# GpSimd takes two of the eight tiles of each residual, and the samples' columns at the entry of a sublayer, in a two-layer decoder step

## The chip, the cores and the metric

One core of a Trainium2 chip runs the whole program. The metric is the device time of one execution in microseconds (us), lower is better. Engines are named as the profile names them: PE (TensorE, PEld its weight loads), DVE (VectorE), ACT (ScalarE), POOL (GpSimd), SP (SyncE, which issues the weight loads from HBM). A name with q is an engine's queue that issues DMAs.

## What is computed

Two layers of a decoder, on 256 prompt tokens and 8 sample tokens (one token each of 8 sequences) with the same weights, model width 1024, all in float32. Each layer has three sublayers, each between a norm at the entry and one at the exit:

```
def sub_in(t, i):
    return rmsnorm(t, norm_pre[i]) * (1.0 + m_scale[:, i, None]) + m_shift[:, i, None]

def sub_out(t, y, i, res):
    return t + res * m_gate[:, i, None] * rmsnorm(y, norm_post[i])

x = sub_out(x, swiglu(sub_in(x, 0), ffn_up[0], ffn_down[0]), 0, FFN_RES)
h = sub_in(x, 1)
...
x = sub_out(x, merged, 1, 1.0)
x = sub_out(x, swiglu(sub_in(x, 2), ffn_up[1], ffn_down[1]), 2, FFN_RES)
```

The middle sublayer projects h, runs two recurrent branches (RWKV-7 and gated DeltaNet) and merges them through w_out. The factors m_scale, m_shift and m_gate come from a conditioning vector: one for the whole prompt, one for each sample.

## The kernel before, in words

**Layout.** The state x is kept transposed in SBUF: xT has 128 partitions and 8 tiles (NT) of 264 columns (T), of which columns 0 to 255 (0:NPR) are the prompt's tokens and the last 8 (NPR:T) the samples'. A row of columns is a token, a partition of a tile one of the 1024 features. y (the output of a sublayer) and h (scratch for squares and scaled tiles) have the same shape. Weights arrive by DMA in a ring of five slots; ACT casts each to w_hi (`high`, line 714), DVE subtracts to get the low part (`low`, line 722), and each product is made of three matmuls (high x high, high x low, low x high), all on line 898.

**Order of work.** Every engine has its own program, written out by hand in the order in which it runs, and semaphores join them: nothing reorders at run time. Per layer: FFN 0, mixing, output projection, FFN 1. Names with "ada" are the matmuls that make the conditioning factors, spread in pieces over the program.

**The exit of a sublayer** (`sub_out(s)` on DVE; s is the sublayer). ACT evicts each output tile from PSUM to y, with the prompt's gate as the scale (`leave`), and squares it; PE sums the squares over the features (`mean_square`), ACT turns the sum into rs = (mean)^-1/2 by Ln and Exp (`normalise`, lines 1491 and 1493). DVE multiplies the samples' columns of y by their gates mod_g, waits for rs (`rs_ready`), and then does two operations for each of the eight tiles, interleaved by one: y = y\*rs, and xT = xT + y, which posts `x_ready`.

**The entry of the next sublayer** (`sub_in(s, hi)` on DVE). ACT squares each tile of xT as it is posted (`square_input`, line 1499), PE sums, ACT makes the new rs. At FFN 1 ACT also casts two weights between the squares and the new rs, and DVE splits them (`ahead`). DVE then makes for each tile scaled_x(j) = xT \* mod_a \* rs into h (256 prompt columns), ACT adds the shift and rounds to the high part hi ("cut", line 1514), and DVE makes the low part h_lo and posts `h_ready`; PE starts on tile k of the sublayer's first two products when h_ready for it is there (`enter`). The samples' eight columns of all tiles go through five operations of their own on DVE, in the buffer y[:, :, NPR:T] (`rows`): times mod_a, times rs, plus the shift, copy to hi, subtract to h_lo. The last four follow rs, and the first h_lo tile stands behind them:

```
tt(rows, rows, bm(rs[:, NPR:T], NT))
...
tt(rows, rows, bias[:, :, 1:NROW], ALU.add)
...
dve.tensor_copy(hi[:, :, NPR:T], rows)
...
tt(h_lo[:, :, NPR:T], rows, hi[:, :, NPR:T].bitcast(F32), ALU.subtract)
```

There are six residuals (three sublayers, two layers) and five entries that follow one; the very first entry has no residual ahead of it. Behind the last residual PE transposes xT back tile by tile (line 2581, and 2582 for the samples), and ACT and its queue write the outputs. `x_ready` counts all tiles, and X_DONE is its last count.

**POOL before.** At the start it sets constants (memsets, selects). Then, in each layer, it only issues DMAs for the mixing: `gather`, `fetch`, `store`, `scatter`, and loads of a recurrent state.

Of the kernel before, what the change touches and what calls it, by code (L numbers as in the profile page):

```python
# [55 lines left out]
X_DONE = 1 + 3 * DEPTH * NT  # L56
# [6 lines left out]
Y_BANKS = (4, 1)  # L63
B16 = 16
CLEAR0, INV0 = (29, 35, 67), (32, 38, 72)
SOLVE = ({21: (1, 4), 23: (4, 7), 24: (7, 10), 26: (10, 12), 27: (12, 15)}, {32: (1, 7), 33: (7, 15)}, {68: (1, 7), 69: (7, 15)})

# [126 lines left out]
def build(nc, I, O):  # L194
    ctx = ExitStack()
    with ctx:
# [532 lines left out]
        with nc.Block() as block:  # L729
# [139 lines left out]
            for l in range(DEPTH):  # L869

                @block.gpsimd
                def _(pool):
# [5 lines left out]

                    for run in range(3):
# [11 lines left out]
                    for g in range(2):  # L891
                        rows = I["state_rwkv_wkv"][l].rearrange("b (j g) v k -> g (b j) (v k)", g=2)[g]
                        pool.dma_start(samp_seen[64 * g:64 * g + 64, :, :].rearrange("p v k -> p (v k)"), rows[:, 2048:4096]).then_inc(samp_in[0].sem, samp_in[0].one())

                @block.tensor
                def _(pe):
# [23 lines left out]
                    def enter(outs, keys, x_hi):  # L920

                        both = [weights((l, *key)) for key in keys]
# [47 lines left out]
                    def mean_square(buf=h):  # L970

                        for k in range(NT):
                            pe.wait_ge(sq_ready.sem, sq_ready.next(pe))
                            i = mm(banks[0][:, 0:T], mean_all[:, :], buf[:, k, :], k == 0, k == NT - 1)
# [4 lines left out]
                    def ffn(i_ffn):  # L979
                        for t in range(FT):  # L980
                            if t == 0:
                                enter([banks[2 * g][:, 0:T] for g in range(2)], [(f"up{i_ffn}", g) for g in range(2)], hi_ffn)
# [45 lines left out]
                    else:  # L1028
                        mean_square()
                    ffn(0)  # L1030
                    mean_square()

                    def dense(t):
                        k = t
                        if k < 2:
                            if k == 0:
                                pe.wait_ge(out_taken.sem, out_taken.at(NT))
                                enter([banks[g][:, 0:T] for g in range(2)], TILES[0:2], hi_in)
# [392 lines left out]
                    mean_square()  # L1431
# [4 lines left out]
                def _(act):  # L1436
# [58 lines left out]
                    def square_input(start=False, m=None, late=False):  # L1495
                        for j in range(NT):
                            if j == 0 or not start:
                                act.wait_ge(x_ready.sem, x_ready.next(act))
                            act.activation(h[:, j, :], xT[:, j, :], ACT.Square).then_inc(sq_ready.sem, sq_ready.one())
                            if m and j == 6:  # L1500
# [479 lines left out]
                def _(dve):  # L1980
# [38 lines left out]
                    def sub_in(s, hi, shift_late=False):  # L2019
# [8 lines left out]
                        tt(rows, xT[:, :, NPR:T], mod_a[:, NT * s:NT * (s + 1), 1:NROW]).then_inc(dve_chain.sem, dve_chain.one())  # L2028
                        dve.wait_ge(dve_chain.sem, dve_chain.all())
# [4 lines left out]
                        tt(rows, rows, bm(rs[:, NPR:T], NT)).then_inc(dve_chain.sem, dve_chain.one())  # L2034
                        for j in range(1, NT if shift_late else 2):
                            scaled_x(j)
                        dve.wait_ge(dve_chain.sem, dve_chain.all())
                        if shift_late:
# [594 lines left out]
```

## Time and profile before

| | |
|---|---|
| time, median of 3 runs | 1984.1 us (1982.7 to 1984.65) |
| the profiled execution | 1987.61 us, its span 1985.9 us |
| mean granted TensorE clock | 0.965 |
| PE busy | 1857.3 us, 94% of the span |
| DVE busy | 1254.2 us, 63% |
| ACT busy | 927.1 us, 47% |
| POOL busy | 76.6 us, 4%, 155 instructions |
| DMA | 353.34 MB, mean 178 GB/s |

A share of busy time is a mean over stages of the program. Line numbers are those of the kernel before; most DVE work goes through two helpers (line 1982 for operations with two tensors, 1985 for those with a scalar per partition too), so groups are told apart by their tiles. A number in brackets at the end of a row is the time that the engine sat idle before it, and what ended that.

### The profile page before, as it was taken

What the parts mean: (1) busy time and instruction counts of PE and PEld (TensorE: products, weight loads), DVE (VectorE), ACT (ScalarE), POOL (GpSimd) and SP (SyncE); (2) the same over time, 40 slices, a digit from 0 to 9 for tenths busy, and PEclk for the clock granted to TensorE, in tenths of its full rate; (3) what the DMA queues carried; (4) which work ended last, traced back from release to release, by engine and by line L of the source; (5) the groups of instructions that cost most, each with busy time, mean ns of one, the idle gap of its engine ahead of it and who ended that gap; (6) DMA issues with size and microseconds to landing.
All of it is one profiled execution on the core that took longest, in us unless ns stands there. A gap on an engine that the chain in (4) does not pass through costs nothing.

```text
span 1985.9 us, 44909 instructions
## 1 busy us (share of the span) xinstructions
PE 1857.3 (94%) x19156; PEld 1685.2 (85%) x19156; DVE 1254.2 (63%) x2187; ACT 927.1 (47%) x1804; POOL 76.6 (4%) x155
## 2 busy tenths in 40 slices
PE   5999989999999888899999999899899998789998
PEld 3899978878888777788989999788799878679997
DVE  3455355776456776688656654577754586769953
ACT  3333455454456544433444444654544764353343
POOL 0000000121000200000000000001200011000000
PEclk7999999999999998999999999999999998899999
DMA  7777765655565664698765666554553555259873
GB/s 261 222 224 225 212 178 168 179 164 151 140 183 155 162 190 122 196 290 271 196 191 150 181 176 184 162 151 142 151 152 101 149 134 141 87 147 275 245 198 110
DMA packets 538085, 353.34 MB, mean 178 GB/s; under 512 B 19620, under 2 KB 515270, under 8 KB 536590
## 3 DMA queue, kind: packets, MB, share of 16 engines
q1 hardware_dynamic: 472202, 302.74, 53.2%
q10 hardware_dynamic: 60756, 38.81, 6.9%
q0 software_dynamic: 4928, 8.92, 1.7%
q8 instruction: 151, 2.47, 0.5%
q14 instruction: 48, 0.39, 0.1%
HBM read 332.27 MB, written 18.50 MB: 177 GB/s over the span
## 4 chain that ended last, share of the span: by engine, by line
PE 76%; DVE 10%; DMA 6%; ACT 4%; issue 3%; POOL 1%; SPq 0%; ACTq 0%; DVEq 0%; POOLq 0%
PE bank L898 73%; DMA ring<-in_w_ada 3%; DMA ring<-in_ffn_up 2%; PE bank L649 2%; DVE ring_r L722 2%; DVE far L1982 1%; ACT w_hi_r L714 1%; DVE y L1982 1%; DVE big L606 1%; DVE big L1982 1%; DVE big L605 1%; POOL far L625 1%; DVE h L1985 1%; DVE big L1985 1%; ACT far L614 0%
## 5 line engine op out<-in xcount | busy, mean ns | idle before, releaser
L898 PE MATMUL bank<-big_r,w_hi_r 128*128 128x264 f32 x4160 | 1074.2, 293 | 43.9 <-DVE h_r L1985 20.9
L898 PE MATMUL bank<-big_r,ring_r 128*128 128x264 f32 (+1 forms) x3456 | 992.1, 287 | 0.0
L898 PEld LDWEIGHTS bank<-big_r,w_hi_r 128*128 128x128 f32 x4160 | 744.8, 190 | 106.9 <-issue 86.0
L898 PE MATMUL bank<-h_r,w_hi_r 128*128 128x264 f32 x2752 | 792.1, 288 | 0.0
L722 DVE TENSOR_TENSOR ring_r<-ring,w_hi_r 128x1024 fp32r<-128x1024 f32 (+2 forms) x440 | 523.8, 1196 | 373.2 <-ACT w_hi_r L714 369.0
L714 ACT CAST w_hi_r<-ring 128x1024 fp32r<-128x1024 f32 (+2 forms) x440 | 452.6, 1029 | 458.7 <-PE bank L898 231.0
L898 PEld LDWEIGHTS bank<-big_r,ring_r 128*128 128x128 f32 (+1 forms) x3456 | 657.9, 190 | 1.1
L898 PEld LDWEIGHTS bank<-h_r,w_hi_r 128*128 128x128 f32 x2752 | 527.9, 192 | 1.6 <-issue 0.5
L898 PE MATMUL bank<-ring,c 128*32 128x256 f32 x1152 | 94.4, 407 | 24.4 <-DMA ring<-in_w_ada 23.9
L898 PE MATMUL bank<-big,far 64*64 64x64 f32 (+2 forms) x1440 | 103.7, 255 | 0.0
L898 PEld LDWEIGHTS bank<-big,far 64*64 64x64 f32 (+1 forms) x1440 | 86.9, 139 | 11.9 <-issue 11.3
L1982 DVE TENSOR_TENSOR big<-big,bank 128x264 f32<-128x264 f32 (+2 forms) x138 | 62.7, 458 | 36.5 <-PE bank L898 24.6
L898 PEld LDWEIGHTS bank<-ring,c 128*32 128x32 f32 x1152 | 24.1, 110 | 55.2 <-DMA ring<-in_w_ada 33.8
L898 PE MATMUL bank<-big 128*64 128x64 f32 (+4 forms) x736 | 52.4, 273 | 18.6 <-DVE big L1982 18.6
L570 POOL DMA_DIRECT2D lt_blocks<-far x48 | 26.9, 568 | 1017.4 <-issue 642.1
L898 PEld LDWEIGHTS bank<-big 128*64 128x64 f32 (+2 forms) x736 | 39.1, 166 | 30.9 <-DVE big L1982 22.1
L649 PE MATMUL bank<-far 64*64 64x48 f32 (+2 forms) x1536 | 54.0, 226 | 9.7 <-DMA far<-t_blocks 8.2
L649 PEld LDWEIGHTS bank<-far 64*64 64x64 f32 x1536 | 51.1, 145 | 13.5 <-DMA far<-t_blocks 8.9
L1985 DVE SCALAR_TENSOR_TENSOR rs<-big,pcol,rs 128x256 f32<-128x256 f32 x78 | 37.8, 485 | 37.3 <-ACT rs L1656 35.1
L898 PE MATMUL bank<-far 64*64 64x64 f32 (+1 forms) x864 | 54.6, 233 | 0.7 <-DVE far L664 0.7
L1599 ACT COPY big<-bank 128x264 f32<-128x264 f32 x48 | 18.2, 380 | 78.1 <-PE bank L898 77.8
L898 PEld LDWEIGHTS bank<-far 64*64 64x64 f32 (+1 forms) x864 | 51.0, 146 | 3.7 <-DVE far L664 0.9
(300 smaller groups left out, 1827.7 us busy)
## 6 DMA issues: line engine op xcount, KB each, us to landing
ring<-in_ffn_up SPq DMA_DIRECT2D x176, 512.0 KB, 4.6
ring<-in_w_in SPq DMA_DIRECT2D x148, 512.0 KB, 3.9
ring<-in_w_ada SPq DMA_DIRECT2D x144, 512.0 KB, 4.3
ring<-in_ffn_down SPq DMA_DIRECT2D x64, 512.0 KB, 3.8
far<-in_state_gdn_ssm ACTq DMA_DIRECT2D x28, 512.0 KB, 5.5
ring<-in_ffn_down SPq DMA_DIRECT2D x32, 384.0 KB, 3.2
ring<-in_w_out SPq DMA_DIRECT2D x16, 512.0 KB, 4.3
out_sample_gdn_ssm<-far ACTq DMA_DIRECT2D x16, 512.0 KB, 4.7
```

What stands on the lines that cost most here:

```text
L570: pool.dma_start(lt_blocks[part_of, :, :].rearrange("u s t -> s u t"), lt[rows, :, cols]).then_inc(block_in.sem, block_in.one())
L605: after(dve.tensor_tensor(p, t_s.to_broadcast([P, rest, s]), t_m[:, s:s + 1, 0:s].to_broadcast([P, rest, s]), ALU.mult))
L606: after(dve.tensor_tensor(below, below, p, ALU.add))
L625: pool.dma_start(into[rows, :, 2 * cols.start:2 * cols.stop], t_blocks[part_of].rearrange("u s t w -> s u (t w)")).then_inc(block_out.sem, ...
L649: i = pe.matmul(out, x_b[hf, u, :] if s else lt[hf, u, :], moving, start=True, stop=True)
L714: act.copy(w_hi[:, m % HI, 0:size], ring[:, slot[n], 0:size]).then_inc(hi_ready.sem, hi_ready.one())
L722: dve.tensor_tensor(ring_r[:, slot[n], 0:size], w, w_hi[:, m % HI, 0:size].bitcast(F32), ALU.subtract).then_inc(lo_ready.sem, lo_ready.one())
L898: return pe.matmul(out, lhsT, rhs, start=start, stop=stop)
L1599: act.copy(qk[:, i - A_TILES, 3:T + 3], src)
L1982: return dve.tensor_tensor(out, a, b, op)
L1985: return dve.scalar_tensor_tensor(out, a, s, b, op0, op1)
```

## The change

In each residual DVE does tiles 0 to 5 (LATE = 6) and POOL tiles 6 and 7, with its own semaphores. At the five entries behind a residual POOL does the five operations on the samples' columns; the first entry keeps them on DVE. ACT and PE take the squares in the order 0, 1, 2, 6, 3, 4, 5, 7. PE's `enter` first waits for POOL's last operation. `pooled(l, what, n)` counts what POOL has posted. The core of the diff:

```
+LATE = NT - 2
+SQUARED = (0, 1, 2, 6, 3, 4, 5, 7)
-X_DONE = 1 + 3 * DEPTH * NT
+X_DONE = 1 + 3 * DEPTH * LATE
...
+                    def residual(s):
+
+                        pool.wait_ge(out_taken.sem, out_taken.at((NT, NT + PROJ + NT, NT + PROJ + 2 * NT)[s]))
+                        ys = y[:, LATE:NT, NPR:T]
+                        pool.tensor_tensor(ys, ys, mod_g[:, NT * s + LATE:NT * (s + 1), 1:NROW], ALU.mult).then_inc(pool_chain.sem, pool_chain.one())
+                        pool.wait_ge(pool_chain.sem, pool_chain.all())
+                        pool.wait_ge(rs_ready.sem, rs_ready.at(2 * s + 2))
+                        for j in range(LATE, NT):
+                            pool.tensor_tensor(y[:, j, :], y[:, j, :], rs[:, :], ALU.mult).then_inc(pool_chain.sem, pool_chain.one())
+                            pool.wait_ge(pool_chain.sem, pool_chain.all())
+                            pool.tensor_tensor(xT[:, j, :], xT[:, j, :], y[:, j, :], ALU.add).then_inc(pool_done.sem, pool_done.one())
+
+                    def rows_in(s, hi):
+
+                        sub = s % 3
+                        rows, bias = y[:, :, NPR:T], modv[:, 3 * NT * sub:3 * NT * sub + NT, 1:NROW]
+
+                        def then(i):
+                            i.then_inc(pool_chain.sem, pool_chain.one())
+                            pool.wait_ge(pool_chain.sem, pool_chain.all())
+
+                        pool.wait_ge(x_ready.sem, x_ready.nth(1 + LATE * (3 * l + s)))
+                        pool.wait_ge(pool_done.sem, pool_done.all())
+                        then(pool.tensor_tensor(rows, xT[:, :, NPR:T], mod_a[:, NT * sub:NT * (sub + 1), 1:NROW], ALU.mult))
+                        pool.wait_ge(rs_ready.sem, rs_ready.at(2 * s + 1))
+                        then(pool.tensor_tensor(rows, rows, bm(rs[:, NPR:T], NT), ALU.mult))
+                        then(pool.tensor_tensor(rows, rows, bias, ALU.add))
+                        then(pool.tensor_copy(hi[:, :, NPR:T], rows))
+                        pool.tensor_tensor(h_lo[:, :, NPR:T], rows, hi[:, :, NPR:T].bitcast(F32), ALU.subtract).then_inc(pool_done.sem, pool_done.one())
+
+                    residual(0)
+                    rows_in(1, hi_in)
                     for run in range(3):
...
+                    residual(1)
+                    rows_in(2, hi_ffn)
+                    residual(2)
+                    if l + 1 < DEPTH:
+                        rows_in(3, hi_ffn)
...
+                    def enter(outs, keys, x_hi, rows=None):
+
+                        if rows:
+                            pe.wait_ge(pool_done.sem, pool_done.nth(rows))
...
-                        for j in range(NT):
-                            if j == 0 or not start:
+                        for n, j in enumerate(range(NT) if start else SQUARED):
+                            if j >= LATE and not start:
+                                act.wait_ge(pool_done.sem, pool_done.nth(pooled(m[0], ("out", m[1]), j - LATE)))
+                            elif n == 0 or not start:
                                 act.wait_ge(x_ready.sem, x_ready.next(act))
...
                         dve.wait_ge(x_ready.sem, x_ready.all())
-                        tt(rows, xT[:, :, NPR:T], mod_a[:, NT * s:NT * (s + 1), 1:NROW]).then_inc(dve_chain.sem, dve_chain.one())
-                        dve.wait_ge(dve_chain.sem, dve_chain.all())
+                        if not shift_late:
+                            dve.wait_ge(pool_done.sem, pool_done.nth(pooled(l if s else l - 1, ("out", (s - 1) % 3), 1)))
...
-                        ys = y[:, :, NPR:T]
-                        tt(ys, ys, mod_g[:, NT * s:NT * (s + 1), 1:NROW]).then_inc(dve_chain.sem, dve_chain.one())
+                        ys = y[:, 0:LATE, NPR:T]
+                        tt(ys, ys, mod_g[:, NT * s:NT * s + LATE, 1:NROW]).then_inc(dve_chain.sem, dve_chain.one())
...
-                        for j in range(NT + 1):
-                            if j < NT:
+                        for j in range(LATE + 1):
+                            if j < LATE:
```

How it moves instructions. DVE before, at the end of layer 0's first residual and the entry to the mixing:

```order
L1982 TENSOR_TENSOR y<-y,rs 128x264
L1982 TENSOR_TENSOR xT<-xT,y 128x264 [waits dve_chain] x2
L1982 TENSOR_TENSOR y<-xT,mod_a 128x8x8 [waits x_ready]
L1985 SCALAR_TENSOR_TENSOR h<-xT,mod_a,rs 128x256 [waits rs_ready,dve_chain]
L1982 TENSOR_TENSOR y<-y,rs 128x8x8
L1985 SCALAR_TENSOR_TENSOR h<-xT,mod_a,rs 128x256
L1982 TENSOR_TENSOR y<-y,modv 128x8x8 [waits dve_chain]
L2044 CAST big_r<-y 128x8x8 [waits dve_chain]
L1982 TENSOR_TENSOR h_r<-y,big_r 128x8x8 [waits dve_chain]
L1985 SCALAR_TENSOR_TENSOR h_r<-h,modv,big_r 128x256 [waits cut_ready]
```

Here big_r holds hi, h_r is h_lo, and modv the shift. The same place on DVE in the changed kernel (its line numbers differ):

```order
L2035 TENSOR_TENSOR y<-y,rs 128x264
L2035 TENSOR_TENSOR xT<-xT,y 128x264 [waits dve_chain] x2
L2038 SCALAR_TENSOR_TENSOR h<-xT,mod_a,rs 128x256 [waits rs_ready,pool_done,x_ready]
L2038 SCALAR_TENSOR_TENSOR h<-xT,mod_a,rs 128x256
L2038 SCALAR_TENSOR_TENSOR h_r<-h,modv,big_r 128x256 [waits cut_ready]
```

The five operations of 128x8x8 have left, and four of the 128x264 ahead of them. They stand on POOL, ahead of the layer's first gather, where before there was no instruction:

```order
L894 TENSOR_TENSOR y<-y,mod_g 128x2x8 [waits out_taken]
L898 TENSOR_TENSOR y<-y,rs 128x264 [waits rs_ready,pool_chain]
L900 TENSOR_TENSOR xT<-xT,y 128x264 [waits pool_chain]
L898 TENSOR_TENSOR y<-y,rs 128x264
L900 TENSOR_TENSOR xT<-xT,y 128x264 [waits pool_chain]
L913 TENSOR_TENSOR y<-xT,mod_a 128x8x8 [waits pool_done,x_ready]
L915 TENSOR_TENSOR y<-y,rs 128x8x8 [waits rs_ready,pool_chain]
L916 TENSOR_TENSOR y<-y,modv 128x8x8 [waits pool_chain]
L917 CAST big_r<-y 128x8x8 [waits pool_chain]
L918 TENSOR_TENSOR h_r<-y,big_r 128x8x8 [waits pool_chain]
L581 DMA lt_blocks<-far 16x16x16 [waits prod_dve]
```

All but one wait for the one in front; only the second y\*rs starts without a wait.

## Rows read from the trace of the kernel before

**Rows 1.** The page: the chain by engine, and the costliest group of instructions

```profile
PE 76%; DVE 10%; DMA 6%; ACT 4%; issue 3%; POOL 1%; SPq 0%; ACTq 0%; DVEq 0%; POOLq 0%
...
L898 PE MATMUL bank<-big_r,w_hi_r 128*128 128x264 f32 x4160 | 1074.2, 293 | 43.9 <-DVE h_r L1985 20.9
```

**Rows 2.** Windows over three of the five edges: length, then busy time per engine

```profile
263.00:278.05 15.05, 10.28 (x59) 6.07 (x58) 9.07 (x29) 6.90 (x17) 0.00 (x0) 1.00 0.69 200
...
1034.50:1047.22 12.72, 8.26 (x48) 3.90 (x46) 9.51 (x31) 6.08 (x14) 0.00 (x0) 0.96 0.54 156
...
1753.00:1767.37 14.37, 6.99 (x24) 3.63 (x24) 10.20 (x27) 7.87 (x16) 0.00 (x0) 0.97 0.28 74
```

**Rows 3.** Timeline, first residual: start us, duration us, engine, line, operation, tiles

```profile
267.34 0.42 ACT L1493 ACTIVATE rs<-rs 128x264 f32<-128x264 f32 x1
...
267.87 0.78 DVE L1982 TENSOR_TENSOR y<-y,rs 128x264 f32<-128x264 f32 x2 [3.46 <-ACT rs L1493]
268.56 0.42 DVE L1982 TENSOR_TENSOR xT<-xT,y 128x264 f32<-128x264 f32 x1
...
269.08 0.42 ACT L1499 ACTIVATE h<-xT 128x264 f32<-128x264 f32 x1 [1.32 <-DVE xT L1982]
...
272.69 0.77 DVE L1982 TENSOR_TENSOR xT<-xT,y 128x264 f32<-128x264 f32 x2
...
273.15 0.77 ACT L1499 ACTIVATE h<-xT 128x264 f32<-128x264 f32 x2 [0.26 <-DVE xT L1982]
```

**Rows 4.** Timeline, the entry behind it, up to the first matmul

```profile
275.33 0.42 ACT L1493 ACTIVATE rs<-rs 128x264 f32<-128x264 f32 x1
275.86 0.49 DVE L1985 SCALAR_TENSOR_TENSOR h<-xT,mod_a,rs 128x256 f32<-128x256 f32 x1 [2.14 <-ACT rs L1493]
...
276.40 0.48 DVE L1985 SCALAR_TENSOR_TENSOR h<-xT,mod_a,rs 128x256 f32<-128x256 f32 x1
276.44 0.98 ACT L1514 ACTIVATE big_r<-h,modv 128x256 fp32r<-128x256 f32 x2 [0.69 <-DVE h L1985]
...
277.28 0.22 DVE L1982 TENSOR_TENSOR h_r<-y,big_r 128x64 fp32r<-128x64 f32 x1
277.42 0.48 DVE L1985 SCALAR_TENSOR_TENSOR h_r<-h,modv,big_r 128x256 fp32r<-128x256 f32 x1
...
278.05 0.44 PE L898 MATMUL bank<-big_r,w_hi_r 128*128 128x264 f32 x1 [3.27 <-DVE h_r L1985]
```

**Rows 5.** Timeline of POOL at the program's start

```profile
3.68 0.32 POOL L757 MEMSET carry<- 128x264 f32 x1
4.06 0.10 POOL L759 MEMSET carry<- 128x4 f32 x1
...
5.19 0.53 POOL L740 TENSOR_SCALAR_AFFINE_SELECT masks<-masks 64x64 f32<-64x64 f32 x2
5.79 0.23 POOL L740 TENSOR_SCALAR_AFFINE_SELECT below<-below 64x48 f32<-64x48 f32 x1
```

**Rows 6.** Timeline, last residual: DVE's adds and PE's transposes of tiles 5 to 7

```profile
1978.52 0.43 DVE L1982 TENSOR_TENSOR xT<-xT,y 128x264 f32<-128x264 f32 x1
...
1979.01 0.68 PE L2581 MATMUL bank<-ident,xT 128*128 128x128 f32 x2
...
1979.70 0.68 PE L2581 MATMUL bank<-ident,xT 128*128 128x128 f32 x2
...
1980.39 0.63 PE L2581 MATMUL bank<-ident,xT 128*128 128x128 f32 x2
```

**Rows 7.** Timeline, entry to layer 0's second FFN: weight splits ahead of the first scaled_x

```profile
806.22 2.36 DVE L722 TENSOR_TENSOR ring_r<-ring,w_hi_r 128x1024 fp32r<-128x1024 f32 x2 [1.24 <-ACT w_hi_r L714]
...
807.48 0.42 ACT L1493 ACTIVATE rs<-rs 128x264 f32<-128x264 f32 x1
808.50 0.48 DVE L1985 SCALAR_TENSOR_TENSOR h<-xT,mod_a,rs 128x256 f32<-128x256 f32 x1
```

**Rows 8.** Windows, behind the first matmul: length, busy per engine, PE clock, DMA share, GB/s

```profile
278.05:281.36 3.31, 3.31 (x15) 3.31 (x16) 3.31 (x9) 2.04 (x4) 0.00 (x0) 0.52 0.00 0
```

More of the change, by code:

```diff
@@ L66, with pooled @@
 SOLVE = ({21: (1, 4), 23: (4, 7), 24: (7, 10), 26: (10, 12), 27: (12, 15)}, {32: (1, 7), 33: (7, 15)}, {68: (1, 7), 69: (7, 15)})
+def pooled(l, what, n=0):
+    steps = [("out", 0), ("out", 0)] + [("in", 1)] * 1 + [("values", 0)] * 0
+    steps += [("out", 1), ("out", 1)] + [("in", 2)] * 1 + [("out", 2), ("out", 2)] + [("in", 3)] * 1
+    kind = ("values", 0) if what == "values" else what
+    return POOL_SETUP + l * len(steps) + steps.index(kind) + (n if what == "values" else steps.count(kind) - 1 if n is None else n) + 1
 class Signal:
@@ L1037, in dense @@
                                 pe.wait_ge(out_taken.sem, out_taken.at(NT))
-                                enter([banks[g][:, 0:T] for g in range(2)], TILES[0:2], hi_in)
+                                enter([banks[g][:, 0:T] for g in range(2)], TILES[0:2], hi_in, pooled(l, ("in", 1)))
                             return
@@ L1430, in _ @@
                     edge_begins(1)
-                    mean_square()
+                    mean_square(order=SQUARED)
                     ffn(1)
@@ L2033, in sub_in @@
                         scaled_x(0)
[L2034 removed]
+                        if shift_late:
+                            tt(rows, rows, bm(rs[:, NPR:T], NT)).then_inc(dve_chain.sem, dve_chain.one())
                         for j in range(1, NT if shift_late else 2):
                             scaled_x(j)
[L2037 removed]
                         if shift_late:
+                            dve.wait_ge(dve_chain.sem, dve_chain.all())
                             for m in range(2):
@@ L2041, in sub_in @@
                             conditioning(0, 1, sel_shift_ready)
-                        tt(rows, rows, bias[:, :, 1:NROW], ALU.add).then_inc(dve_chain.sem, dve_chain.one())
-                        dve.wait_ge(dve_chain.sem, dve_chain.all())
-                        dve.tensor_copy(hi[:, :, NPR:T], rows).then_inc(dve_chain.sem, dve_chain.one())
-                        dve.wait_ge(dve_chain.sem, dve_chain.all())
-                        tt(h_lo[:, :, NPR:T], rows, hi[:, :, NPR:T].bitcast(F32), ALU.subtract)
+                            tt(rows, rows, bias[:, :, 1:NROW], ALU.add).then_inc(dve_chain.sem, dve_chain.one())
+                            dve.wait_ge(dve_chain.sem, dve_chain.all())
+                            dve.tensor_copy(hi[:, :, NPR:T], rows).then_inc(dve_chain.sem, dve_chain.one())
+                            dve.wait_ge(dve_chain.sem, dve_chain.all())
+                            tt(h_lo[:, :, NPR:T], rows, hi[:, :, NPR:T].bitcast(F32), ALU.subtract)
                         for j in range(NT):
```

25 lines of the change are left out of this document (16 added, 9 removed).

## The prediction

> **What bounds the kernel now.** I read the page first, its chain and its groups: TensorE (PE) carries 76% of the chain that ended last, VectorE (DVE) 10%, and the largest group of matmuls sat idle 43.9 us, of which it waited 20.9 us for the tile h_r that DVE writes [rows 1]. So most of the span is PE work that this change doesn't touch, and DVE is on the path only in places. The places are the six residuals and the five entries behind them. The windows view, laid over the stretch from the last matmul of one sublayer to the first of the next, gives 12.7 to 15.1 us for each of the five, with PE busy in only half to two thirds of it [rows 2]. The timeline of the first one shows why: it is a chain with nothing beside it.
>
> Residual: the factor rs is ready at 267.34 + 0.42 = 267.76. DVE starts at 267.87 and issues 16 operations of 128x264, eight y\*rs and eight xT+y, at a pace of (5.59 - 0.43)/15 = 0.344 us (an operation lasts 0.43, the next starts before it ends), and ends at 272.69 + 0.77 = 273.46. ScalarE (ACT) squares each tile 0.04 us behind its add; the first adds leave gaps, the last two squares run together and the last one starts at about 273.50 [rows 3]. Entry: PE sums the squares, ACT makes the new rs (ready 275.75), DVE starts the first scaled_x at 275.86, and the first matmul of the sublayer comes at 278.05, 2.30 us behind rs [rows 4]. In these 2.3 us the five small operations on the samples' columns stand between the scaled tiles and the first h_lo, of which four come behind rs. Behind the first matmul PE is the slower side: it runs for 3.31 us at a granted clock of 0.52 (the 1.2 GHz level, after a stretch in which it only summed squares), busy all the time [rows 8]. So what matters is when it starts.
>
> **The change, part by part.** GpSimd (POOL) does nothing at these places now, so only the new work counts there. Its DMAs are issued in the same order, and those of the mixing wait for things that come microseconds behind an entry; I cost that at nothing. The small gate operations on the samples (y\*mod_g) run before rs is ready, on DVE and on POOL: nothing.
>
> *(a) Four of sixteen operations leave DVE, in each of six residuals.* DVE's last add ends at 267.87 + 11 x 0.344 + 0.43 = 272.08. The square of tile 5 follows at 272.12, that of tile 7, now last, 0.35 later: 272.47 for 273.50, **-1.03 us**, if POOL is done by then and DVE keeps its pace. In the last residual the adds feed transposes, and those take 0.69 us a tile even where the tile is long there (1979.70, 1980.39) [rows 6]. PE is as slow as DVE there, so I take -0.1 without a slower DVE, and -0.35 (one slot, for tile 5) as the start from which delays count.
>
> *(b) The same four operations on POOL, in a chain.* No row has POOL with two inputs. Bounds for one of 128x264: 0.32 us, its memset of that size, which only writes; and 0.75 us, three accesses (two reads, one write) at the memset's slope of (0.32 - 0.10)/260 = 0.82 ns a column, 3 x 264 x 0.82 = 0.65, and its fixed 0.10 [rows 5]. I take 0.6, nearer the upper, since operations that read are slower in the same rows than memsets. With a gap of 0.07 four take 2.7 us and end near 270.6, before DVE. POOL's own length thus costs nothing; tile 7 is in time up to (272.43 - 267.91)/4 = 1.13 us each.
>
> *(c) Both engines read SBUF at the same moment.* This is the term that decides and that no row shows. All 12 operations left on DVE and all 4 on POOL read two operands from SBUF. Call d the delay that one POOL operation puts on DVE's row of operations. At least 0: they run side by side. At most 0.75 + 0.08 = 0.83: DVE waits for the whole operation and loses its own overlap of 0.43 - 0.344. A residual costs -1.03 + 4d, the last one -0.35 + 4d, so the whole change is zero near d = 0.2, one quarter of the interval. I take **d = 0.5**: the two take turns, and DVE waits for the part of POOL's 0.6 in which it moves data (less the fixed 0.10). Five residuals: 5 x (-1.03 + 2.0) = +4.85; the last: +1.65.
>
> The Trainium skill ("SBUF — State Buffer", section "Who interferes with whom") says of this that a VectorE instruction with two SBUF inputs contends with a GpSimd instruction that reads SBUF, and that the one which starts second "fully blocks"; no run here shows it. By that rule alone d would be at its upper part; without it the sum would be that of the first rival.
>
> *(d) The samples' operations at five entries.* Four leave the 2.30 us. On DVE the path is then scaled_x (start +0.11, 0.49), ACT's cut (start 276.44, 0.69 behind rs, 0.51 long by half of the pair's 0.98 and its overlap), h_lo (0.48), and PE 0.15 behind it: 0.69 + 0.51 + 0.48 + 0.15 = 1.83, or **-0.47**. PE now waits for POOL's last one as well. POOL's four, at the pace of its select of 64x64 (0.30 [rows 5]), take 1.2: side by side they are hidden. In turns, each may wait for a DVE operation of 0.48: at worst 0.11 + 1.2 + 1.92 + 0.15 = 3.38, +1.1. I take half of the waits: 0.26 + 1.2 + 0.96 = 2.42, and DVE's path, delayed by two of POOL's, is 1.83 + 0.60 = 2.43: **+0.15**, five times +0.75.
>
> *(e) The waits.* At the second FFN's entry DVE now waits for POOL's tile 7 ahead of its two weight splits; these wait for ACT's casts, which come behind all squares anyway [rows 7]. They move with (a): DVE is the last there (808.50, rs was ready at 807.90), and the chain is as long as before. ACT and PE take tile 6 fourth; at 0.35 us a square it fits a gap.
>
> The sum: 4.85 + 1.65 + 0.75 = **+7.25 us**. The profiled execution took 1987.61 us (1.7 of it outside the span of 1985.9); it would become 1994.9. It stood 3.5 above the median of the runs, 1984.1, and against that the prediction is 1991.4. Ends: side by side 5 x (-1.03 - 0.47) - 0.1 = -7.6; whole blocking 5 x (2.29 + 1.08) + 2.97 = +19.8.
>
> **The rivals.** A measurement of this kernel tells from no change about 0.2%, 4 us.
>
> *Side by side.* d = 0, all of (a) and (d) is gained: 1976.5. For it: POOL is idle, each engine keeps to other columns, and nothing in the profile shows one disturbing the other. Against it: nothing shows them reading together either. It decides at d under 0.2, and is the rival that ends on the other side.
>
> *POOL is the bound.* They run side by side, but an operation takes POOL over 1.13 us, and tile 7 and the samples' columns come last: at 1.39 each ((273.46 - 267.91)/4) a residual gains nothing, and an entry nothing at 0.51 for a small one. At 1.3 and 0.5 the time is 5 x -0.36 - 0.1 = -1.9, 1982.2. Against it: it needs more than the 0.75 of my upper bound; for it: a first two-input operation on POOL after hundreds of microseconds of DMA issuing is a case that no row shows.
>
> *Given back.* The 1 to 1.5 us of an edge are regained or lost elsewhere, since the weights come no earlier. Against it: the loads of the next tiles are in before the entry starts, and PE is busy without a break behind it [rows 8]. I count it into the second rival's middle.
>
> **How the numbers follow.** Taking turns 0.50, side by side 0.32, POOL the bound or given back 0.18. Of the first, slower by over 4 us (d above 0.36 or so) 0.42, within it 0.07, faster 0.01; of the second, faster 0.28, within 0.04; of the third, within 0.11, slower 0.06, faster 0.01. So faster 0.30, same 0.22, slower 0.48. The range goes from just under the side-by-side value, 1976, to 2001 (+17; most of the way to whole blocking), which leaves out some 0.08 at each end. The likeliest case alone would be 1985 to 2001.
>
> **What would show it.** In the changed profile: the pace of DVE's operations in a residual while POOL works (0.344 now; about 0.34 + 0.5 per POOL operation if they take turns); POOL's lengths (0.6, or stretched to over 1); the start of the last square behind rs (5.74 now; 6.7 by the forecast, 4.71 side by side); the first matmul behind the second rs (2.30 now; 2.45, or 1.83); its releaser, POOL or DVE; and the last add of DVE against POOL's. The prediction is wrong if DVE's pace stays 0.344 with POOL beside it.

## The result, and the profile of the changed kernel

The changed kernel takes 1995.4 us (median of 19 runs, 1987.6 to 2002.1) against 1984.1 (19 runs, 1975.3 to 1992.7): the ratio is **1.0065 [1.0051, 1.008]**, slower by 10 to 16 us. The profiled execution took 1991.18 us, its span was 1989.5. The page, as [rows 1]:

```profile
PE 72%; DVE 12%; DMA 6%; ACT 5%; issue 3%; POOL 1%; ACTq 1%; SPq 0%; DVEq 0%; POOLq 0%
...
L946 PE MATMUL bank<-big_r,w_hi_r 128*128 128x264 f32 x4160 | 1071.5, 292 | 43.5 <-DVE ring_r L733 13.1
...
L946 PE MATMUL bank<-h,mean_all 128*128 128x264 f32 x160 | 53.6, 498 | 11.5 <-ACT h L1552 11.5
```

DVE has a larger share of the chain, 12% for 10%. PE's idle time in the large group is the same, 43.5 for 43.9 us, but h_r no longer ends most of it. So the loss isn't in that group. It shows in the timeline of the first residual, as [rows 3], its columns the same:

```profile
266.63 0.42 ACT L1544 ACTIVATE rs<-rs 128x264 f32<-128x264 f32 x1
...
267.16 1.32 DVE L2035 TENSOR_TENSOR y<-y,rs 128x264 f32<-128x264 f32 x2 [3.42 <-ACT rs L1544]
267.21 0.99 POOL L898 TENSOR_TENSOR y<-y,rs 128x264 f32<-128x264 f32 x1 [3.53 <-ACT rs L1544]
268.27 0.82 POOL L900 TENSOR_TENSOR xT<-xT,y 128x264 f32<-128x264 f32 x1
268.41 0.97 DVE L2035 TENSOR_TENSOR xT<-xT,y 128x264 f32<-128x264 f32 x1
...
270.06 0.81 POOL L900 TENSOR_TENSOR xT<-xT,y 128x264 f32<-128x264 f32 x1
270.19 0.97 DVE L2035 TENSOR_TENSOR xT<-xT,y 128x264 f32<-128x264 f32 x1
271.08 0.42 DVE L2035 TENSOR_TENSOR y<-y,rs 128x264 f32<-128x264 f32 x1
...
271.67 6.35 PE L946 MATMUL bank<-h,mean_all 128*128 128x264 f32 x14 [1.01 <-ACT h L1552]
...
272.80 0.77 DVE L2035 TENSOR_TENSOR xT<-xT,y 128x264 f32<-128x264 f32 x2
273.25 1.08 ACT L1552 ACTIVATE h<-xT 128x264 f32<-128x264 f32 x3 [0.26 <-DVE xT L2035]
...
278.06 0.48 ACT L1542 ACTIVATE rs<-bank,epsc 128x264 f32<-128x264 f32 x1 [3.72 <-PE bank L946]
```

While POOL works, DVE's operations last 0.97 us instead of 0.42 and follow each other by 0.89 instead of 0.344. The sixth starts at 271.08, 3.92 us behind the first, where it would start after 5 x 0.344 = 1.72: the four POOL operations delay DVE by 2.2 us, 0.55 each. From there on the pace is 0.344 again. The last add ends at 272.80 + 0.77 = 273.57, 6.51 behind rs (ready at 267.05) for 5.70 before, the squares at 274.33. Then comes what the prediction didn't hold: ACT's next operation waits 3.72 us for PE's sums (0.90 before), and starts 11.01 behind the first rs, where it started 7.06 behind it. The windows over the stages of this edge show what changed for PE (length, PE, its weight loads, DVE, ACT and POOL busy, granted clock, DMA share, GB/s):

```profile
267.16:271.67 4.51, 1.35 (x10) 0.46 (x11) 4.51 (x7) 0.85 (x2) 3.51 (x4) 0.91 0.95 264
271.67:278.05 6.38, 6.35 (x14) 4.49 (x14) 1.90 (x6) 2.20 (x6) 0.32 (x1) 0.53 0.25 87
278.05:281.11 3.06, 0.00 (x1) 0.03 (x1) 1.78 (x4) 1.82 (x4) 1.32 (x4) 1.00 0.00 0
281.11:284.40 3.29, 3.29 (x15) 3.29 (x16) 3.29 (x9) 2.05 (x4) 0.00 (x0) 0.50 0.00 0
```

PE worked 1.35 of the 4.51 us in which the slowed DVE released two tiles, and then summed at a granted clock of 0.53 (most of it at the 1.2 GHz level). In the same stretch of the other four edges the clock was 0.55, 0.58, 0.68 and 0.64. Before, it was 1.00 while PE summed (270.00 to 275.30).

The entry, as [rows 4], and the entry to the last FFN:

```profile
279.14 1.05 DVE L2038 SCALAR_TENSOR_TENSOR h<-xT,mod_a,rs 128x256 f32<-128x256 f32 x2 [5.57 <-ACT rs L1544]
279.14 0.32 POOL L915 TENSOR_TENSOR y<-y,rs 128x64 f32<-128x64 f32 x1 [5.18 <-ACT rs L1544]
...
280.37 0.32 POOL L918 TENSOR_TENSOR h_r<-y,big_r 128x64 fp32r<-128x64 f32 x1
280.38 0.59 DVE L2038 SCALAR_TENSOR_TENSOR h_r<-h,modv,big_r 128x256 fp32r<-128x256 f32 x1 [0.19 <-ACT big_r L1567]
...
281.11 0.54 PE L946 MATMUL bank<-big_r,w_hi_r 128*128 128x264 f32 x1 [3.09 <-DVE h_r L2038]
...
1767.22 0.39 PE L946 MATMUL bank<-big_r,w_hi_r 128*128 128x264 f32 x1 [3.24 <-POOL h_r L918]
```

Here rs is ready at 278.99 and the first matmul follows 2.12 us later (2.30 before). At both entries to the second FFN POOL ends last and the first matmul comes 2.26 us behind rs (2.78 before; there DVE shares the time with two weight splits). POOL's groups:

```profile
L898 POOL TENSOR_TENSOR y<-y,rs 128x264 f32<-128x264 f32 x12 | 11.5, 962 | 21.3 <-ACT rs L1544 21.3
...
L900 POOL TENSOR_TENSOR xT<-xT,y 128x264 f32<-128x264 f32 x12 | 9.7, 811 | 0.9
```

The five edges, from the first rs to the first matmul of the next sublayer, take 14.06, 14.00, 13.46, 12.63 and 13.08 us (10.29, 11.65, 10.29, 10.27 and 11.64 before): **+13.1 us**. Of these 5 x 1.12 = 5.6 lie ahead of the end of the squares, 9.0 between that and the start of ACT's Ln (the time of PE's sums; at a second FFN ACT's casts also lie in it), and 3 x -0.18 + 2 x -0.51 = -1.6 behind the second rs. In the last residual DVE ends only 0.82 us later, but from rs to the end of the span it is 13.4 for 11.6 us, and PE's transposes are slow from the first on:

```profile
1978.38 0.69 PE L2641 MATMUL bank<-ident,xT 128*128 128x128 f32 x2 [3.42 <-DVE xT L2035]
...
1980.16 0.69 PE L2641 MATMUL bank<-ident,xT 128*128 128x128 f32 x2 [0.88 <-DVE xT L2035]
```

Before, the first four pairs had lasted 0.44 and only the later ones 0.63 to 0.69. In all +14.9 us by the rows, for the measured 10 to 16. The two profiled spans differ by 3.6 only: between two edges there are hundreds of microseconds that this change doesn't touch, and they vary. The longest such stretch (first to second edge) took 521.0 us in the profile of before, 512.0 in that of after, and 513 to 523 in those of the experiments below. So each edge is read in the profile and the total in the repeated runs.

### The profile page after: what moved, and what is told of

The parts are those of the page before. It is cut to its first block, busy times and chain, and to the rows that moved or that the text cites. A ratio compares the mean times of both kernels' runs of the same rounds, so it can differ in the third digit from the quotient of the medians.

```text
span 1989.5 us, 44936 instructions
## 1 busy us (share of the span) xinstructions
PE 1845.7 (93%) x19156; PEld 1676.8 (84%) x19156; DVE 1255.0 (63%) x2138; ACT 926.9 (47%) x1804; POOL 108.6 (5%) x210
## 4 chain that ended last, share of the span: by engine, by line
PE 72%; DVE 12%; DMA 6%; ACT 5%; issue 3%; POOL 1%; ACTq 1%; SPq 0%; DVEq 0%; POOLq 0%
PE bank L946 70%; DMA ring<-in_ffn_up 3%; DMA ring<-in_w_ada 2%; DVE ring_r L733 2%; PE bank L660 2%; DVE y L2035 1%; ACT w_hi_r L725 1%; DVE big L2035 1%; DVE far L2035 1%; DVE big L617 1%; POOL far L636 1%; DVE big L616 1%; ACTq L1918 1%; DVE h L2038 1%; DVE big L2038 1%
## 5 line engine op out<-in xcount | busy, mean ns | idle before, releaser
L946 PE MATMUL bank<-big_r,w_hi_r 128*128 128x264 f32 x4160 | 1071.5, 292 | 43.5 <-DVE ring_r L733 13.1
L946 PE MATMUL bank<-h,mean_all 128*128 128x264 f32 x160 | 53.6, 498 | 11.5 <-ACT h L1552 11.5
L946 PEld LDWEIGHTS bank<-h,mean_all 128*128 128x128 f32 x160 | 38.4, 250 | 25.9 <-ACT h L1552 17.6
## 6 DMA issues: line engine op xcount, KB each, us to landing
ring<-in_ffn_up SPq DMA_DIRECT2D x176, 512.0 KB, 4.6
ring<-in_w_in SPq DMA_DIRECT2D x148, 512.0 KB, 3.9
ring<-in_w_ada SPq DMA_DIRECT2D x144, 512.0 KB, 4.3
ring<-in_ffn_down SPq DMA_DIRECT2D x64, 512.0 KB, 3.7
far<-in_state_gdn_ssm ACTq DMA_DIRECT2D x28, 512.0 KB, 6.1
ring<-in_w_out SPq DMA_DIRECT2D x16, 512.0 KB, 4.4
out_sample_gdn_ssm<-far ACTq DMA_DIRECT2D x16, 512.0 KB, 4.9
```

The costliest lines, as they stand in the source:

```text
L946: return pe.matmul(out, lhsT, rhs, start=start, stop=stop)
```

## The experiments

The theory after this result was: DVE and POOL hold each other up when both read SBUF; the slowed DVE leaves gaps in PE's work; PE's clock falls, and the sums are slow. The rivals: the entries or PE's added wait cost the time; the cost lies in POOL working at all, whatever it reads; the lower clock comes along with the loss and costs nothing itself. Where an edge is measured below, it runs from the first rs ready to the first matmul; the five together took 54.1 us before and 67.2 after the change.

### Each half of the change alone

Residuals alone: POOL keeps its two tiles, DVE takes the samples' operations back, and PE's wait goes.

```diff
                     residual(0)
-                    rows_in(1, hi_in)
...
                     residual(1)
-                    rows_in(2, hi_ffn)
                     residual(2)
-                    if l + 1 < DEPTH:
-                        rows_in(3, hi_ffn)
```

> The change with the residuals' part alone: POOL takes tiles 6 and 7 of each residual, the samples' columns at the entries are back on DVE. Theory (the loss lies in the residual: DVE and POOL take turns at reading, and the longer gaps let PE's clock fall while it sums the squares): DVE's first five operations of a residual still take 3.9 us instead of 1.7, the last square ends about 7.3 us behind rs, the sums end late (new factor started 9.6 to 11 us behind rs, 7.06 before), and the entry is as before, 2.30 us from the second rs to the first matmul (2.78 at the second FFN). Sum of the edges' excess 15 to 17 us, ratio 1.006 to 1.009. Rival (PE's wait for POOL at the entry makes the loss): edges as before and ratio within 0.2% of 1.

Measured: **1.0072 [1.0046, 1.0099]** (8 runs against 29). The edges sum to 66.0 us, DVE ends 6.50 and the squares 7.27 us behind rs, as with the whole change; behind the second rs it is 2.29 again at three entries. With the last residual (13.7 for 11.6) the excess is 14.0 us, just under the 15 to 17 expected. One of its edges, the second, tells the delay and the clock apart. There matmuls for the conditioning factors ran in the gap, PE's clock stayed at 1.00, and the sums of equally late squares were fast:

```profile
797.75:802.37 4.62, 2.39 (x27) 0.62 (x19) 4.51 (x7) 0.85 (x3) 3.51 (x4) 1.00 0.62 177
...
802.37 3.67 PE L941 MATMUL bank<-h,mean_all 128*128 128x264 f32 x14 [1.01 <-ACT h L1546]
...
806.82 0.47 ACT L1536 ACTIVATE rs<-bank,epsc 128x264 f32<-128x264 f32 x1
```

The fourteen matmuls take 3.67 us where they took 6.14 in the changed kernel's second edge, and Ln starts 1.79 us behind the end of the squares, as in the kernel before (there ACT's casts end last in both; in the changed kernel it is 3.50).

Entries alone: all eight tiles stay on DVE, POOL does the samples' operations.

```diff
-LATE = NT - 2
-SQUARED = (0, 1, 2, 6, 3, 4, 5, 7)
+LATE = NT
+SQUARED = (0, 1, 2, 3, 4, 5, 6, 7)
...
-                    residual(0)
                     rows_in(1, hi_in)
```

> The change with the entries' part alone: all eight tiles of a residual on DVE, the five small operations on the samples' columns on POOL. Theory (residual makes the whole loss): residual and sums as before (last square ends 6.16 us behind rs, PE at full clock while it sums), the first matmul follows the second rs by 2.12 us instead of 2.30, and by 2.26 instead of 2.78 at the second FFN: 1.5 us in all, ratio 0.999, not to be told from 1. Rival (POOL's small operations and PE's wait for them cost something): edges longer than before, ratio above 1.002.

Measured: **1.0002 [0.9984, 1.002]** (10 against 29). The edges sum to 53.1 us, 1.1 less than before; the first matmul comes 2.12 us behind rs (2.51 at the second FFN, where 2.26 was expected). So the whole loss comes with the residuals. The entries gain about 1 us, which a total can't show.

### POOL beside DVE on spare data

What does POOL's work cost DVE, if it is no part of the computation's chain? The kernel before, with four extra operations on POOL beside the first residual of each layer, from the constant tile carry into a spare buffer. The output is the same.

```diff
+                    pool.wait_ge(rs_ready.sem, rs_ready.at(2))
+                    for j in range(4):
+                        i = pool.tensor_tensor(svx[:, 0:T], carry[:, :], carry[:, :], ALU.mult)
...
+                                pe.wait_ge(pool_done.sem, pool_done.nth(4 + l))
                                 enter([banks[g][:, 0:T] for g in range(2)], TILES[0:2], hi_in)
```

> The kernel before, and beside each layer's first residual POOL does four operations of 128x264 with two inputs in SBUF (constants into a spare place, results unused), each waiting for the one in front; DVE keeps all 16 operations. Theory (turns at reading): DVE loses 0.5 to 0.6 us per POOL operation, so its last add ends 7.9 us behind rs instead of 5.70, and POOL's operations take 0.8 to 1.0 us. Rival (what slows DVE is that both work on the same tiles and semaphores of the residual): DVE ends at 5.70.

The second kernel has `pool.tensor_copy(svx[:, 0:T], carry[:, :])` in that place, which reads one operand:

> As beside_tt_b, with copies of 128x264 (one input in SBUF). If any read by POOL makes DVE's two-input operations wait, DVE ends 0.2 to 0.5 us later per copy, so between 6.5 and 7.7 us behind rs, less than beside two-input operations because a copy is shorter. Rival (only POOL's second input collides): 5.70.

The third has `pool.memset(svx[:, :], 1.0)`, 896 columns each, which only writes:

> As beside_tt_b, with memsets of 128x896 (no input, written data only, some 0.85 us each by the slope of the memsets at the program's start). Theory (the collision is in reading): DVE ends at 5.70 us behind rs, as if POOL were idle. Rival (any POOL operation that touches SBUF blocks DVE): 3 us later.

The timelines of the three, two inputs first:

```profile
266.31 2.95 POOL L881 TENSOR_TENSOR svx<-carry 128x264 f32<-128x264 f32 x4 [260.14 <-ACT rs L1501]
266.33 1.67 DVE L1990 TENSOR_TENSOR y<-y,rs 128x264 f32<-128x264 f32 x2 [3.46 <-ACT rs L1501]
267.92 0.85 DVE L1990 TENSOR_TENSOR xT<-xT,y 128x264 f32<-128x264 f32 x1
...
269.47 0.42 DVE L1990 TENSOR_TENSOR xT<-xT,y 128x264 f32<-128x264 f32 x1
```

One input:

```profile
266.12 2.05 POOL L881 COPY svx<-carry 128x264 f32<-128x264 f32 x4 [259.95 <-ACT rs L1501]
266.16 1.20 DVE L1990 TENSOR_TENSOR y<-y,rs 128x264 f32<-128x264 f32 x2 [3.46 <-ACT rs L1501]
267.28 0.62 DVE L1990 TENSOR_TENSOR xT<-xT,y 128x264 f32<-128x264 f32 x1
...
268.38 0.42 DVE L1990 TENSOR_TENSOR xT<-xT,y 128x264 f32<-128x264 f32 x1
```

None:

```profile
266.70 3.55 POOL L881 MEMSET svx<- 128x896 f32 x4 [260.61 <-ACT rs L1501]
266.75 0.78 DVE L1990 TENSOR_TENSOR y<-y,rs 128x264 f32<-128x264 f32 x2 [3.46 <-ACT rs L1501]
267.44 0.42 DVE L1990 TENSOR_TENSOR xT<-xT,y 128x264 f32<-128x264 f32 x1
```

DVE's last add ends 7.44, 6.53 and 5.69 us behind rs, against 5.70 without POOL, and the same to 0.01 us in the second layer. So an operation of two inputs delays DVE by 1.75/4 = 0.44 us, one of one input by 0.21, and a memset by nothing, though four of them keep POOL busy for 3.55 us. The first two delays are smaller than expected (0.5 to 0.6 for two inputs), and so are POOL's own operations: 0.63 to 0.70 us with two inputs, which are here one and the same tile, where 0.8 to 1.0 was expected, and 0.40 to 0.49 for a copy. There is one run of each, and their times of 1986.9, 1978.4 and 1978.5 us are inside the spread of single runs (before: 1977.5 to 1988.9) and settle nothing. The delay doesn't come from POOL working, and it doesn't need the residual's own tiles: it comes with POOL's reads.

### The clock: filler for PE in the gaps

The changed kernel, with seven matmuls on constants into an unused bank, four ahead of PE's wait for the first square and three ahead of the second.

```diff
                         for n, k in enumerate(order):
+                            for _ in range((4, 3)[n] if fill and n < 2 else 0):
+                                mm(banks[1][:, 0:T], mean_all[:, :], carry[:, :], True, True)
                             pe.wait_ge(sq_ready.sem, sq_ready.next(pe))
```

> The changed kernel with seven more matmuls on PE at each entry (constants, into a free bank, results unused): four ahead of the first square and three ahead of the second, so that PE has work in the gaps that slower squares leave. Theory (of the 15 us that the edges lose, about 9 come from PE's clock, which fell to 0.5 while it waited between squares): with the gaps filled the granted clock stays at 1.00 while PE sums, the new factor starts about 0.9 us behind the last square instead of 2.3 to 3.7, edges lose 5 to 7 us in all and the ratio is 1.002 to 1.004. Rival (the sums are slow for another reason, the extra matmuls only add work): the sums stay slow and the ratio is 1.006 or more.

Measured: **1.0074 [1.0052, 1.0096]** (10 against 29). Windows over the first edge and the 5 us behind it:

```profile
267.21:279.08 11.87, 7.54 (x42) 5.80 (x39) 8.19 (x16) 4.85 (x13) 5.15 (x9) 0.97 0.50 152
279.08:284.08 5.00, 5.00 (x23) 5.00 (x24) 4.82 (x13) 3.27 (x7) 0.00 (x0) 0.50 0.00 0
```

The clock in the five edges is 0.97, 1.00, 1.00, 0.99 and 0.87 (0.72 to 0.86 without the filler), the squares end as late as before (7.28), and Ln starts 8.3 to 9.8 us behind rs instead of 9.6 to 11.0. The edges sum to 61.3 us, 5.9 less than with the change alone. So the low clock did make the sums slow. That 5.9 and not all 9.0 us come back is at least in part the filler's own doing: in the second edge the second square is there at 805.00, but its sum starts at 806.96, behind the filler. Ln was expected 0.9 us behind the last square and starts 1.0 to 2.6 behind it.

But the time didn't follow. The ratio is what the rival forecast, and the lower end of its interval, 1.0052, is above what the edges would give, (14.9 - 5.9)/1984 = 0.45%. The gain isn't lost right behind the entries, although at two of them (the fourth and fifth) PE ran at 1.00 in the changed kernel and at 0.68 and 0.66 with the filler: from an edge's first Ln to ACT's first weight cast behind its entry the five edges together take 89.1 us before, 101.4 with the change and 95.5 with the filler. At that cast all of the 5.9 us are still there. Whether and where they are lost later, these runs don't settle.

### DVE reads one operand from PSUM

If the delay is in reads of SBUF, it should go when DVE reads only one of its two operands there. In five of the six residuals ACT writes the factor into PSUM too (banks[1]), DVE puts y\*rs into three free banks in turn, and adds from there. POOL keeps its tiles and reads SBUF. The last residual stays as it was.

```diff
+                            act.activation(banks[1][:, 0:T], rs[:, :], ACT.Exp, scale=-0.5).then_inc(rs_ready.sem, rs_ready.one())
+                            act.activation(rs[:, :], rs[:, :], ACT.Exp, scale=-0.5).then_inc(rs_ready.sem, rs_ready.one())
...
-                                tt(y[:, j, :], y[:, j, :], rs[:, :]).then_inc(dve_chain.sem, dve_chain.one())
+                                tt(product[j], y[:, j, :], factor).then_inc(dve_chain.sem, dve_chain.one())
...
-                                tt(xT[:, j - 1, :], xT[:, j - 1, :], y[:, j - 1, :], ALU.add).then_inc(x_ready.sem, x_ready.one())
+                                tt(xT[:, j - 1, :], xT[:, j - 1, :], product[j - 1], ALU.add).then_inc(x_ready.sem, x_ready.one())
```

> The changed kernel, but in five of the six residuals (all but the last) no DVE operation has two operands in SBUF: ACT writes the factor rs to a PSUM bank first and to SBUF behind it, DVE writes y*rs to PSUM banks and adds from there. POOL's part is unchanged. Theory (DVE and POOL wait for each other only because both read two operands from SBUF): DVE keeps a pace of 0.34 to 0.42 us per operation while POOL works, the last square ends 5.2 to 5.9 us behind rs (6.16 in the kernel before, 7.28 in the changed one), PE keeps its clock, and the ratio to the kernel before is 0.996 to 1.000. Rival (any operation of POOL beside DVE slows it, whatever DVE reads): the first five operations take 3.9 us as now, ratio 1.006 or more.

Measured: 0.9989 [0.9972, 1.0006] (10 against 29). The timeline of the first residual:

```profile
266.50 0.78 DVE L2042 TENSOR_TENSOR bank<-y,bank 128x264 f32<-128x264 f32 x2 [3.39 <-ACT bank L1576]
266.88 0.74 POOL L898 TENSOR_TENSOR y<-y,rs 128x264 f32<-128x264 f32 x1 [3.83 <-ACT rs L1577]
267.18 0.42 DVE L2042 TENSOR_TENSOR xT<-xT,bank 128x264 f32<-128x264 f32 x1
...
268.58 3.85 PE L946 MATMUL bank<-h,mean_all 128*128 128x264 f32 x16
...
269.90 0.76 DVE L2042 TENSOR_TENSOR xT<-xT,bank 128x264 f32<-128x264 f32 x2
...
272.47 0.48 ACT L1542 ACTIVATE rs<-bank,epsc 128x264 f32<-128x264 f32 x1 [1.04 <-PE bank L946]
```

DVE's pace beside POOL is 0.340 us, and POOL takes 0.74 and 0.75 an operation, reading the same tiles from SBUF. The last add ends 3.92 us behind the SBUF rs, the sums run at a clock of 1.00, and Ln starts 5.73 behind rs (7.06 before, 11.01 after the change). The edges sum to 46.2 us, counted from the SBUF rs. That one is ready 0.33 us behind the PSUM one, so this count leaves out 1.7 us over five edges. A second set of runs, since the interval included no change:

> The same kernel as psum_after_b, to see whether its gain over the kernel before is real: edges 6 us shorter, ratio 0.997 with an interval below 1 if the edges' gain reaches the end; within 0.1% of 1 if it is given back.

Measured: 0.9982 [0.9962, 1.0003] (10 against 21). One edge, 10.69 us, was longer: PE waited for the weights of an ada piece.

The control has the same operands in PSUM and no work on POOL: the kernel before with the two edits above, over all eight tiles.

> The kernel before with the PSUM operands of psum_after_b and without any work on POOL: a control. Theory (PSUM operands only make room for POOL, DVE's pace is the same): DVE's 16 operations at 0.344 us, last add 5.5 us behind the first operation, ratio 0.999 to 1.001. Rival (the gain of psum_after_b comes from the PSUM operands themselves): edges shorter by over 1 us each, as there.

Measured: 1.0003 [0.9986, 1.0021] (10 against 13), DVE's pace 0.340. The edges sum to 53.3 us by the same count (one of them, 11.14, had late weights too). So PSUM as an operand gains nothing by itself. It takes away what POOL costs, and then POOL's share of the work shortens the edges by 7.1 us against this control. In the time the two sets with POOL, 0.9989 and 0.9982, don't show that gain clear of no change, each by itself.

### The same at the entries: the fastest version

DVE's scaled_x also reads two operands from SBUF, while POOL does the samples' columns. Here the entry's factor goes to PSUM too.

```diff
-                            stt(h[:, j, 0:NPR], xT[:, j, 0:NPR], mod_a[:, NT * s + j, 0:1], rs[:, 0:NPR],
+                            stt(h[:, j, 0:NPR], xT[:, j, 0:NPR], mod_a[:, NT * s + j, 0:1], banks[3][:, 0:NPR],
```

> As psum_after_b, and the factor rs of the entries is in PSUM too, so that scaled_x no longer reads two operands from SBUF beside POOL's small operations. Theory: the first scaled_x takes 0.48 us again, h_lo follows earlier and the first matmul comes 1.9 us behind the SBUF copy of the second rs's Exp start-to-end as before, or 0.2 to 0.3 us earlier per edge than in psum_after_b, unless POOL's last small operation (1.7 us behind rs) is then the later one; edges 6 to 8 us shorter in all than in the kernel before, ratio 0.996 to 0.999. Rival (gain of the edges is given back in the stages behind them): edges shorter and ratio 1.000 or more.

Measured: **0.9972 [0.9955, 0.999]** (12 against 21; 1975.7 us for 1982.0). The first matmul comes 1.65 to 1.70 us behind the SBUF rs, 2.09 and 2.34 at the second FFNs. The edges sum to 45.9 us. This beats both the kernel before and the changed one: the whole of split residuals, samples' operations on POOL and factors in PSUM is worth having. There is no control with the entries' factor in PSUM and POOL idle, so the last step's own share isn't shown. The windows of its first entry, 5 us and the 15 behind them:

```profile
275.19:280.19 5.00, 5.00 (x29) 5.00 (x30) 4.82 (x13) 3.44 (x7) 0.00 (x0) 0.68 0.00 0
280.19:295.19 15.00, 14.40 (x121) 12.59 (x122) 8.12 (x12) 10.44 (x21) 0.00 (x0) 1.00 0.73 211
```

### Is the low clock behind an entry worth anything?

The fastest version, with six filler matmuls behind each edge's sums, while ACT and DVE prepare the entry.

```diff
                         mean_square(order=SQUARED)
+                        warm()
                     ffn(0)
```

> The kernel of psum_all with six more matmuls on PE behind the sums of each of the five later entries (constants, into a free bank, results unused; 0.47 us each at full clock), in the 3 us in which PE waits for the factor and the first tile. Theory (PE's clock falls behind an entry because PE stood still ahead of it, as it fell within the sums of the changed kernel): the granted clock of the first 5 us behind the first matmul is over 0.9 instead of 0.66, 1.5 us less per edge, ratio 0.993 to 0.996. Rival (the clock falls whatever PE does there, or the extra matmuls run at the low clock themselves and delay the first real one): the stretch behind stays at 0.66 or the first matmul comes up to 2.6 us later, ratio 0.998 to 1.004.

Measured: 1.0006 [0.9986, 1.0026] (12 against 17), against 0.9972 without the filler. The same windows:

```profile
276.52:281.52 5.00, 5.00 (x40) 4.99 (x41) 4.82 (x13) 3.45 (x7) 0.00 (x0) 1.00 0.00 0
281.52:296.52 15.00, 13.13 (x111) 11.36 (x111) 8.19 (x12) 10.44 (x22) 0.00 (x0) 1.00 0.75 211
```

The forecast of 0.993 to 0.996 failed. The clock is 1.00 behind all five entries and PE gets through 40 matmuls instead of 29 in the 5 us. But in the next 15 us it is busy for 13.1 instead of 14.4: it arrives earlier at weights that come no sooner. Their preparation starts with DVE's last h_lo tile, ACT's load of a function table and its first cast, and from an edge's first Ln to that cast it is 83.2 us over the five edges, 81.9 without the filler. The edges themselves are 1.6 us longer (47.5), none of it behind the filler: in the first one PE waited for the weights of an ada piece, and in the fifth it had stood still for 2.72 us and then summed at a clock of 0.71. The clock was made full and nothing was won. Why it rather came out slower than the fastest version (the intervals overlap, on another chip) stays open, as with the filler above.

## Why the prediction was right or wrong

The sign and the case were right: the engines hold each other up at SBUF, and the kernel is slower. It came out at 1995.4 for 1991.4 us, +11.3 in the medians (10 to 16 by the ratio) for +7.25. That it is so near is in part luck: the sum lacks a term larger than itself, and the time fell inside the range because the range reached up to nearly whole blocking, which is not what happened. By its steps:

- **(c), the deciding term, held.** The delay per POOL operation was put at 0.5 us within 0 to 0.83; it is 0.55 in this kernel and 0.44 on spare data. The start of the last square was forecast 6.7 us behind rs and is 6.9. Five residuals up to the squares' end: +4.85 forecast, +5.6 measured. The Trainium skill ("SBUF — State Buffer", section "Who interferes with whom") says that a VectorE instruction with two SBUF inputs contends with a GpSimd instruction that reads SBUF, not with one that only writes, and that with at most one SBUF input, outside its 2-port modes, it doesn't contend. The traces agree on each: 0.44 and 0.21 us a POOL operation for two inputs and one, 0 for a memset, 0 with an operand in PSUM. The "fully blocks" that the prediction quotes is more than they show: a POOL operation of 0.89 us delays DVE by 0.55, not by its whole length, and a DVE operation comes through every 0.89 us, so the two engines pass alternately.
- **(a) left a term out, and it is the largest.** It gave a residual as -1.03 + 4d, counted to the start of the last square, as if the sums ended as soon behind it as before. They don't: the same delay opens gaps between the squares, PE's clock falls (to 0.53 to 0.68 over the sums), and these cost 9.0 us more over five edges. That the sums were slow because of the clock is shown twice: with filler in the gaps the edges are 5.9 us shorter, with squares as late as in the changed kernel, and where the clock stayed at 1.00 by itself (the second edge of the residuals alone) they cost nothing more. [Rows 8] had shown the pattern at the entry already (clock 0.52 after a stretch in which PE only summed squares), and the prediction read it for the matmuls behind the entry and put the sums ahead of it at nothing.
- **(a), last residual:** the forecast was +1.65, from one saved slot and 4 x 0.5. DVE's end moved by less, -4 x 0.344 + 2.2 = +0.82. The span's end moved by +1.8, and PE, with gaps ahead of it, transposes at the long times nearly throughout; that this is the reason was not tested. The term was near for another reason than its own.
- **(b)** was sized too low: 0.74 to 0.75 us for a POOL operation beside a DVE that doesn't contend, 0.81 and 0.96 in the changed kernel, for 0.6. The upper bound, worked out as three accesses at the memset's slope, came nearest. As forecast, POOL's length costs nothing: POOL is done 3.82 us behind rs, DVE 6.51.
- **(d) had the wrong sign:** -0.18 at three entries and -0.51 at two, for +0.15 at each. The prediction gave POOL half of its possible waits for DVE (0.96 us) and delayed DVE by two of POOL's operations (0.60). In the first entry POOL's small ones last 0.31 to 0.37 us and delay DVE by little: scaled_x and the first h_lo last 0.53 to 0.60 instead of 0.48. (Its own sum, 2.43 for 2.30, is +0.13 and not +0.15.)
- **(e)** held: no wait of the new ones shows on the path but PE's for POOL at the second FFN.
- **The rivals.** "Side by side" is what the kernel does once an operand is in PSUM; its value, -7.6 us, lies within what the fastest version shows, -5.5 (-8.9 to -2.0), whose last residual is left as in the changed kernel. In the changed kernel it did not come: it needed a d under 0.2, and d is 0.55. "Given back" is seen in part: in the fastest version an earlier entry did reach the total, while the faster sums under the filler, and a faster PE behind the entry, did not. "POOL is the bound" did not come: it needed over 1.13 us an operation, and the longest took 1.00.

Two errors of opposite sign are in the sum: 9.0 us of slow sums that it lacks, and entries that it put 2.3 us too high. Without the slow sums the rows would give +5.9, just under the forecast. What stays open is why both kernels with filler are slower than their edges say, by some 5 us: 14.7 for 9.0 with the filler between the squares, +1.2 for about -4 with the other. So the edges show the clock's 9.0 us, and no total by itself does.

## What to carry to other kernels

Before work is moved from VectorE to GpSimd to run beside it, look where both read: if VectorE's instructions take two operands from SBUF, each reading GpSimd instruction cost them about half of its own length here (0.21 of 0.47 us, 0.44 of 0.68, 0.55 of 0.89), and one operand in PSUM removed that. Then follow the delay through to PE: a producer that was slower for 4 us left gaps behind which PE's clock was nearly halved for the following sums, and on the edges that cost more than the delay itself. And price a gain only where the next stage can take it: a faster PE behind the entry was stopped by the next weights.

## What the runs showed of the hardware that was not expected

- The delay grows with the number of operands that POOL reads: 0, 0.21 and 0.44 us for none, one and two of 264 columns. POOL's own operations took 0.63 to 0.70 us beside a contending DVE where both inputs were the same tile, 0.74 and 0.75 beside a DVE that doesn't contend with two different ones, and 0.81 to 1.00 in the changed kernel. How much of that is contention and how much the operands, no run here tells.
- Gaps in PE's work came ahead of the fall, not one long standstill: PE worked 1.35 of 4.51 us, and the next 6.4 us ran at 0.53. It doesn't always fall then: in the run of the residuals alone PE worked 2.39 of 4.62 us, and the clock stayed at 1.00. The filler of seven matmuls held it at 0.97 to 1.00 in four edges, and the 5 us behind the entries ran at 0.50 to 0.68. Nor does it take a slow DVE: in the last kernel's fifth edge, with DVE at its full pace, the sums ran at 0.71.
- A higher clock doesn't have to show in the time at all: at 1.00 for 0.66 to 0.68 behind five entries, no gain was measured.
